# Two hand-written schedules moved inside a fused Trainium2 kernel: where five gate sums stand, and where a convolution's taps and Silu stand

## The reference

```
h  = rms_norm(x) * (1 + scale) + shift          # shift, scale, gate = split(silu(c) @ w_mod + b_mod)
u, g = split(h @ pool_w_in)
pooled = window_mean(u) - u                     # four groups of 512 channels, windows 2, 4, 8, 16
y  = (einsum(pooled, w_grp) * pool_scale * silu(g)) @ pool_w_out
x  = rms_norm(x + gate * y) * final_norm_g

q, k, v, z, a, b = split(rms_norm(x) @ a_w_in)  # 16 heads of 128
q, k, v = silu(causal_conv4(q, k, v))           # 4 taps per channel
o  = gated_deltanet(l2(q), l2(k), v, decay(a), sigmoid(b))   # a triangular solve per chunk of 64
x  = x + (rms_norm(o) * silu(z)) @ a_w_out
x  = x + banded_attention(rms_norm(x)) @ b_w_out
```

## Time and profile before

| | |
|---|---|
| time, median of 3 runs | 1447.68 us (1447.68 to 1451.34) |
| the profiled execution | 1447.68 us, of which the span of its instructions is 1445.9 us |
| PE busy | 1418.4 us, 98% |
| DVE busy | 911.7 us, 63% |
| ACT busy | 739.7 us, 51% |
| POOL busy | 138.5 us, 10% |
| DMA | 303.81 MB, mean 210 GB/s |
| mean granted PE clock | 0.998 of full |

### The profile page before, as it was taken

One profiled execution on the slowest core, in us unless ns is written; L12 is line 12 of the kernel. 1 busy time (PEld: TensorE's weight loads), 2 busy tenths in 40 slices (PEclk: granted clock), 3 DMA queues, 4 the chain that ended last, 5 costly groups with the idle time before them and its releaser, 6 DMA issues.

```text
span 1445.9 us, 25884 instructions
## 1 busy us (share of the span) xinstructions
PE 1418.4 (98%) x10542; PEld 1328.4 (92%) x10542; DVE 911.7 (63%) x1075; ACT 739.7 (51%) x871; POOL 138.5 (10%) x148
## 2 busy tenths in 40 slices
PE   5999998999999999999999999999999999999998
PEld 2446998999999999999999999999999998999998
DVE  3748798775476677679856646645655646556542
ACT  2205344454676675733546564546556555456431
POOL 0000021000050313102133300000000000000000
PEclk9999999999999999999999999999999999999999
DMA  9998799765356454545654657545545555555552
GB/s 386 417 408 347 277 391 384 246 204 196 121 202 204 144 187 152 176 169 184 198 160 147 187 178 228 178 152 195 181 157 172 167 172 189 174 174 169 171 186 73
DMA packets 77722, 303.81 MB, mean 210 GB/s; under 512 B 8704, under 2 KB 8832, under 8 KB 73152
## 3 DMA queue, kind: packets, MB, share of 16 engines
q1 hardware_dynamic: 67104, 261.30, 52.1%
q0 software_dynamic: 10528, 41.19, 8.1%
HBM read 291.97 MB, written 12.58 MB: 211 GB/s over the span
## 4 chain that ended last, share of the span: by engine, by line
PE 85%; DMA 7%; DVE 4%; ACT 3%; issue 1%; SPq 1%; ACTq 0%; DVEq 0%
PE acc L611 20%; PE acc L613 20%; PE acc L614 20%; DMA raw<-weights 4%; PE misc L667 3%; PE acc L667 3%; PE misc L901 2%; PE acc L623 2%; PE acc L622 2%; PE acc L624 2%; DMA mod_ring<-mod_w 1%; PE misc L791 1%; DVE w_lo L1460 1%; ACT w_hi L1072 1%; PE misc L802 1%
## 5 line engine op out<-in xcount | busy, mean ns | idle before, releaser
L1460 DVE TENSOR_TENSOR w_lo<-raw,w_hi 128x1024 fp32r<-128x1024 f32 x392 | 478.2, 1239 | 336.9 <-ACT w_hi L1072 334.5
L1072 ACT ACTIVATE w_hi<-raw 128x1024 fp32r<-128x1024 f32 x392 | 405.8, 1054 | 339.0 <-PE acc L614 197.0
L611 PE MATMUL acc<-b_hi,w_hi 128*128 128x256 f32 x1856 | 532.8, 287 | 5.8 <-DVEq L1601 5.8
L614 PE MATMUL acc<-b_hi,w_lo 128*128 128x256 f32 x1856 | 526.1, 283 | 0.0
L613 PE MATMUL acc<-b_lo,w_hi 128*128 128x256 f32 x1856 | 526.1, 283 | 0.0
L611 PEld LDWEIGHTS acc<-b_hi,w_hi 128*128 128x128 f32 x1856 | 357.0, 192 | 6.6 <-DVEq L1601 6.0
L613 PEld LDWEIGHTS acc<-b_lo,w_hi 128*128 128x128 f32 x1856 | 357.2, 192 | 0.5
L614 PEld LDWEIGHTS acc<-b_hi,w_lo 128*128 128x128 f32 x1856 | 356.8, 192 | 0.0
L611 PE MATMUL acc<-a_hi,w_hi 128*128 128x256 f32 x896 | 254.3, 284 | 0.0
L614 PE MATMUL acc<-a_hi,w_lo 128*128 128x256 f32 x896 | 253.6, 283 | 0.0
L613 PE MATMUL acc<-a_lo,w_hi 128*128 128x256 f32 x896 | 253.6, 283 | 0.0
(11 more groups left out here) (229 smaller groups left out, 1583.0 us busy)
## 6 DMA issues: line engine op xcount, KB each, us to landing
raw<-weights SPq DMA_DIRECT2D x392, 512.0 KB, 4.2
mod_ring<-mod_w SPq DMA_DIRECT2D x26, 1024.0 KB, 12.5
u_ring<-weights SPq DMA_DIRECT2D x32, 512.0 KB, 12.6
gate_ring<-weights POOLq DMA_DIRECT2D x32, 512.0 KB, 7.7
mod_late<-mod_w SPq DMA_DIRECT2D x6, 1024.0 KB, 5.1
xres<-x_t SPq DMA_DIRECT2D x4, 512.0 KB, 16.0
xres<-x_t POOLq DMA_DIRECT2D x4, 512.0 KB, 7.0
x_d<-xres POOLq DMA_DIRECT2D x1, 2048.0 KB, 10.7
```

The lines of the kernel that those rows point to most:

```text
L611: nc.tensor.matmul(to, wh[:, ch], xh, start=kt == 0 and m % 2 == 0, stop=False, skip_group_check=True)
L614: last = nc.tensor.matmul(to, wl[:, ch], xh, start=False, stop=end and m % 2 == 1, skip_group_check=True)
L1072: nc.scalar.activation(w_hi[:, m.c % HL_SLOTS], raw[:, q.c % RAW_SLOTS], ACT.Copy).then_inc(own.up(s_hi), 1)
L1460: nc.vector.tensor_tensor(w_lo[:, slot], raw[:, q.c % RAW_SLOTS], w_hi[:, slot].bitcast(F32), ALU.subtract).then_inc(own.up(s_lo), 1)
```

## The change

Two schedules are edited; no arithmetic is added or removed. One: `gate_behind` is computed instead of listed. Gates 0 to 25 stay behind slabs 14 to 39. Gate 26 moves from slab 47 to slab 40, gate 27 from 48 to 49, gate 29 stays behind 51 and gate 28 behind 50, gate 30 moves from 53 to 52, gate 31 from 54 to 53. Two: the taps and Silu of v. DVE's taps of v groups 0 and 1 move into the section of group 18 (steps 0 and 4, all twelve instructions each), those of v2 into section 19, and those of v3 are halved between sections 20 and 21. ACT's `first_tap_v` and `silu_v` follow, and the Silu of v3 comes last, in section 22 in front of the Silu of z.

```diff
--- before.py
+++ after.py
@@ -153,8 +153,8 @@
 def gate_behind(n):
 
-    late = {47: 26, 48: 27, 50: 28, 51: 29, 53: 30, 54: 31}
-    return n - N_GATE if N_GATE <= n < N_GATE + 26 else late.get(n)
+    k = n - N_GATE if n < N_GRP + 9 else n - N_GATE - 8 if n >= N_GRP + 17 else -1
+    return k if 0 <= k < GATES else None
@@ -1320,18 +1320,23 @@
                 if j >= 0:
                     nc.scalar.activation(t4[:], wide(vo, BATCH * j), ACT.Square).then_inc(own.up(s_sq2), 1)
-                if g == G_A + 10:
-                    first_tap_v(0)
+                if g in (G_A + 10, G_A + 12):
+                    first_tap_v({10: 0, 12: 3}[g - G_A])
                 for k in range(8):
-                    if g == G_A + 10 and k == 5:
+                    if g == G_A + 10 and k == 3:
                         silu_v(0)
+                        first_tap_v(1)
+                    if g == G_A + 10 and k == 7:
+                        silu_v(1)
                     if g >= G_A + 11 and g < G_AOUT - 1 and k:
                         solve_copies(j + 1, k - 1)
-                    if j in (-1, 0, 1) and k == 1:
-                        first_tap_v(j + 2)
-                    if j in (-1, 0, 1) and k == 6:
-                        silu_v(j + 2)
+                    if g == G_A + 11 and k == 1:
+                        first_tap_v(2)
+                    if g == G_A + 11 and k == 6:
+                        silu_v(2)
                     if j >= 0 and k == (0 if last else 1):
+                        if j == 2:
+                            silu_v(3)
                         act.wait_ge(s_zr, j + 1)
                         nc.scalar.activation(gate_z[:], gate_z[:], ACT.Silu).then_inc(own.up(s_zs), 1)
@@ -1797,10 +1802,9 @@
-            V_TAPS = {(G_A + 10, 2): (0, range(GM))}
-            for v in range(1, 4):
-                V_TAPS[G_A + 10 + v, 2] = (v, range(0, 2))
-                V_TAPS[G_A + 10 + v, 4] = (v, range(2, 4))
+            V_TAPS = {(G_A + 10, 0): (0, range(GM)), (G_A + 10, 4): (1, range(GM)),
+                      (G_A + 11, 2): (2, range(0, 2)), (G_A + 11, 4): (2, range(2, 4)),
+                      (G_A + 12, 4): (3, range(0, 2)), (G_A + 13, 4): (3, range(2, 4))}
```

## The result

| | before | after |
|---|---|---|
| time, median (lowest to highest, executions) | 1447.68 us (1446.81 to 1451.34, 4) | 1460.25 us (1459.02 to 1460.61, 4) |
| profiled execution, its span | 1447.68, 1445.9 us | 1458.85, 1457.1 us |
| mean granted PE clock | 0.998 | 0.994 |

The ratio is 1.0081, with a 95% interval of 1.0062 to 1.0099. The change makes the kernel slower. On a second chip, with 23 executions of before and 6 of after, it was 1.0059 (1.0041 to 1.0077), 8.2 us; why it is less there comes with the last two experiments.

The account below looks back on a forecast made before the run. PE's own work, busy 98% of the span, was taken as the bound. Gate stop 5.4 + copy stop 5.2 + low clock 2.1 = 12.7 us on 1447.7 gave 1460.4, stated as 1460; 8-in-10 range 1453 to 1464.5.

Parts of the forecast that it names:

- Edit one: PE's stop before grp product 2: gate 26 behind slab 40 waits for its load, +5.4 us (+1.8 to +7.1).
- rival D: Not slower because gate 26 lands by 246.3: only its sum, +1.2 us, no second stop; 1448.9 us, chance 0.05.
- The clock at the first stop: Before grp product 2: the longer stop loses 2.1 us once, as the shorter did; no difference (-1 to +1).
- Edit two: Section 18: `w_lo`, load, `w_hi` and copy come late; PE stops before solve step 1, +5.2 us (3.2 to 7.7).
- The 0.7 us for POOL's mask ahead of v0's taps: Section 18, DVE: POOL's mask product running in front of the taps of v0 adds 0.7 us.
- The 1.3 us for one of POOL's masks: Section 18: one POOL mask instruction, 1.30 us, gets in ahead of DVE's `w_lo` of k = 4.
- The clock at the second stop: Behind the stop before solve step 1: the clock falls again, +2.1 us (bounds 0 and +3).
- The rest of edit two: Sections 19 to 22: the moved taps and Silu cost 0; up to 0.5 us in section 22 if not hidden.
- Rival C: Solve groups 20 to 22: ACT paces them, so lighter sections make it 7.1 us faster, 1440.6 us; chance 0.03.
- B: Only the gate costs, 5.4 us, with no stop from section 18: 1453.1 us; chance 0.10.
- A: Both stops come, the second short and warm: 5.4 + 3.2 = 8.6 us, 1456.3 us; chance 0.20.
- The 0.7 us of slack: Before solve step 1: ACT's copy ends at 702.80, PE takes the step up at 703.51 without a stop.

Follow-up runs that it names:

- the last two experiments: The changed kernel and the kernel before, each run once more unchanged with a second profile: 1458.95 us, 1.0059, and 1450.16 us, 0.9998.
- e1: The kernel before with only the new `gate_behind`: 1455.06 us, 1.0023 of before.
- e3: e1 with gates 26 and 27 loaded earlier, into the buffers of x's first two reloads, which go behind them: 1449.59 us, 0.9988 of before.
- e4: e2 with the Silu of v1 moved behind the solve's first copy on ACT: 1455.52 us, 1.003 of before.
- e9: e2 with the first copy of solve(0) ahead of the `w_hi` of section 19, k = 0: 1454.02 us, 1.0025 of before.
- e2: The changed kernel with the old `gate_behind`, so only the taps and Silu are moved: 1454.86 us, 1.0027 of before.
- e5: e2 with DVE's taps of v1 one `w_lo` later, behind that of k = 4: 1453.85 us, 1.0024 of before.
- e6: e2 with both the Silu of v1 behind the copy and the taps of v1 one `w_lo` later: 1453.65 us, 1.0014 of before.

## Why the prediction came out, point by point

The forecast was 1460.0 us; after took 1460.25 and 1458.95. The mechanism was the one named. That the number is met to 0.25 us is luck: the sum gave 12.7 us between two profiled executions that were 11.2 us apart, and the median of after lay 1.4 us above its profiled one.

**Edit one: right.** Expected +5.4 us on the stop, by a landing at 250.46. In the first profile the stop grew by 5.9 us and the data came at 250.3; in e1, with section 18 as before, the stop is 11.0 us. The load was issued 1.4 us earlier than in the earlier trace rows and took 8.65 us instead of 7.4, so that it landed at nearly the same time; that the two cancelled is luck (in the second profile it took 7.62). Expected 4.2 us of wait on DVE, measured 5.33, since DVE came there earlier. e3 confirms that the wait is the cost; the sum of 1.2 us alone is not to be seen in the time. By that, rival D had its mechanism right (an early load makes the gate nearly free), but its condition, a landing within 3.2 us, was not met.

**The clock at the first stop: right.** 20 matmuls in 4.41 us, 0.22 us each, as in the earlier trace rows; no difference between the two.

**Edit two: the path right, one term wrong.** Expected a stop of 5.2 us, found 4.1, with the copy released just as chained (`w_lo` of k = 4, 3.4 us of load, `w_hi`, copy). e4 shows that ACT's share is nothing, e9 that this stop goes when the copy no longer stands behind the waiting `w_hi` (in its one profile; the median hardly moved). The 3.4 us of load were right, though the earlier trace rows gave them for the two loads before this one; this one took 3.8 in that profile. The 0.7 us for POOL's mask ahead of v0's taps came: 5.46 against 4.81. The 1.3 us for one of POOL's masks let in ahead of `w_lo` of k = 4 didn't: the four `w_lo` took 4.63 us, 1.16 each, and it was POOL that was held up:

```profile
705.85 7.07 POOL L559 TENSOR_TENSOR t<-l_x,consts 128x512 f32<-128x512 f32 x2 [13.23 <-PE misc L901]
```

against 3.31 us in the earlier trace rows. The rule weighed in the prediction is that of the Trainium skill, SBUF — State Buffer, section "Who interferes with whom": two operands in SBUF make VectorE contend with GpSimd's reads, and, as it says of VectorE's two-port modes, whoever issues first has the shared ports for the whole instruction. The trace agrees that where the two overlap one of them runs long, at either place. What the rule leaves open is who goes next after a whole instruction, and here it was mostly DVE: POOL's row begins at 705.85, while the last of the taps ran, and it lasted through the four `w_lo`, none of which was longer than usual. In the other profiles with both sets of taps ahead it took 6.8 to 7.1 us. That the ports are the reason is argued from the overlap and not tested. Without the term the sum is 3.9 us.

**The clock at the second stop: right.** Expected 2.1 us, step 1 lost 5.47 - 3.57 = 1.9, with the granted clock at 0.50 in 714 to 716.

**The rest of edit two at 0: right.** PE has no wait on the solve after step 1, and group 21 lasts 40.00 us. Rival C falls by this and by e2, and B by e2; A was nearer on the stop's size (it had 3.2, the forecast 5.2, found 4.1) but wrong on its clock. Two readings in rival C were wrong, without weight for the sum. Two gates leave the slabs before 49 and not three (the 2.4 us are right for two). And the change has not one table load fewer: both traces have 15 of them between 600 and 900 us, since the Silu of z in section 21 now needs one of its own.

**The sum.** 5.9 + 4.1 + 1.9 = 11.9 us of a span difference of 11.2; PE's waits at the very start were 1.4 us shorter after than before, so that some 0.7 us stay unaccounted for. What the prediction didn't see is that its starting point, 1447.7 us, was at the low end of what the kernel before takes. Measured against the usual 1450.8 us the loss is 8.2 us, 4.5 less than the 12.7 forecast: of the stops it adds, before has a part already in its second profile (3.0 us). The 0.7 us of slack read from the earlier trace rows was the slack of one execution, and its sign changes in another.

## What to carry to other kernels

A task that is moved to an earlier place costs what its data's landing says, not what its work says: look up when its load is issued, and what frees the buffer. Where a wait in one engine's order stands in front of something short that another engine needs, the load in front of it sets the time; move the short thing ahead, and then look for the next consumer, which may be late as well. Before a slack of a microsecond is used in a sum, take a second profile of the same kernel: if the path runs through a DMA, the slack is one draw from several. And a load that is issued sooner does not land sooner by as much when others are under way.

## What the runs showed of the hardware

- Landings of one and the same load differ by more than some of the edits here: the slab load in front of the copy took 3.8 and 4.92 us in two executions of before, 3.3 to 3.4 in the five profiles in which it was issued late, and 5.79 in e5. The load of gate 26 took 8.65 and 7.62 us in two executions of after.
- When DVE issues one two-operand instruction after another, POOL can be held up at length: two instructions that took 3.31 us in before's first profile took 6.8 to 8.0 in the seven profiles in which the taps of v1 stand in section 18. A POOL instruction that was under way when DVE began its twelve taps made them take 5.46 us and not 4.81.
- Behind PE's stops of 3.4 us (e5), 3.9 (e2) and 4.1 (after, e4) before step 1 the granted clock was 0.50, and step 1 took 5.46 or 5.47 us in the first three of these kernels. It stayed at 1.00 behind those of 1.6 us (before's second profile) and 2.2 (e6).
